# Gated layers: hidden activations of blocks 1 to 8 turned by 32x32 blocks on VectorE and exchanged through DRAM, instead of transposed on TensorE

## The reference

```python
D_FF = 2816
def _swiglu(x, w_in, w_out):
    g, u = jnp.split(x @ w_in, 2, axis=-1)
    return (jax.nn.silu(g) * u) @ w_out

h = _swiglu(_rms_norm(x, ffn1_pre_norm[l]), ffn1_w_in[l], ffn1_w_out[l])
x = x + 0.5 * _rms_norm(h, ffn1_post_norm[l])
m = _token_mixing(...)
x = x + _rms_norm(m, mix_post_norm[l])
h = _swiglu(_rms_norm(x, ffn2_pre_norm[l]), ffn2_w_in[l], ffn2_w_out[l])
x = x + 0.5 * _rms_norm(h, ffn2_post_norm[l])
```

## Time and profile before

| what | us |
|---|---|
| median of 3 runs | 1209.76 (1209.64 to 1209.85) |
| span of the profiled execution, first to last instruction | 1207.9 |
| median less span (start and end around the instructions) | 1.9 |
| TensorE matmul busy | 1197.5 (99%) |
| VectorE busy | 950.9 (79%) |
| ScalarE busy | 622.3 (52%) |
| GpSimd busy | 84.8 (7%) |
| moved by the transfers | 274.31 MB, mean 227 GB/s |
| granted TensorE clock, mean | 0.998 |

### The profile page before, as it was taken

One profiled execution on the slowest core, in us unless ns is written; L12 is line 12 of the kernel. 1 busy time (PEld: TensorE's weight loads), 2 busy tenths in 40 slices (PEclk: granted clock), 3 DMA queues, 4 the chain that ended last, 5 costly groups with the idle time before them and its releaser, 6 DMA issues.

```text
span 1207.9 us, 14813 instructions
## 1 busy us (share of the span) xinstructions
PE 1197.5 (99%) x5798; PEld 983.4 (81%) x5798; DVE 950.9 (79%) x1382; ACT 622.3 (52%) x851; POOL 84.8 (7%) x133
## 2 busy tenths in 40 slices
PE   9999999999999999999999999999999999999997
PEld 7888888888778888888887778888888788888885
DVE  7799868876766689888786668898898878765656
ACT  7445337445774363434465667444446576643441
POOL 2110130000300011000000000000100000000000
PEclk9999999999999999999999999999999999999999
DMA  9999996644645489899566437788856544566640
GB/s 317 347 337 322 307 302 192 218 142 154 203 152 174 152 297 355 309 328 316 172 208 206 139 105 263 271 304 280 309 196 241 192 141 139 177 219 214 188 161 35
DMA packets 145685, 274.31 MB, mean 227 GB/s; under 512 B 6336, under 2 KB 76432, under 8 KB 145616
## 3 DMA queue, kind: packets, MB, share of 16 engines
q1 hardware_dynamic: 127568, 209.73, 51.7%
q0 software_dynamic: 17888, 63.57, 15.4%
q10 hardware_dynamic: 160, 0.07, 0.0%
HBM read 270.41 MB, written 2.93 MB: 226 GB/s over the span
## 4 chain that ended last, share of the span: by engine, by line
PE 94%; DVE 2%; ACT 2%; issue 1%; DVEq 0%
PE ps L532 24%; PE ps L534 24%; PE ps L533 24%; PE ps L865 7%; PE ps L864 3%; PE ps L784 2%; PE ps L732 1%; PE ps L611 1%; ACT hi_w L1194 1%; PE ps L1081 1%; PE ps L738 1%; PE ps L1060 1%; PE ps L942 1%; PE ps L1058 1%; ACT area L1511 1%
## 5 line engine op out<-in xcount | busy, mean ns | idle before, releaser
L1707 DVE TENSOR_TENSOR lo_w<-w_raw,hi_w 128x2048 fp32r<-128x2048 f32 x194 | 440.9, 2286 | 60.9 <-ACT hi_w L1194 60.5
L1194 ACT ACTIVATE hi_w<-w_raw 128x2048 fp32r<-128x2048 f32 x195 | 370.2, 1915 | 51.4 <-DMA w_raw<-in_ffn_w_in 18.6
L532 PE MATMUL ps<-hi_w,xT 128*128 128x512 f32 x848 | 339.4, 400 | 0.0
L534 PE MATMUL ps<-lo_w,xT 128*128 128x512 f32 x848 | 331.3, 391 | 0.0
L533 PE MATMUL ps<-hi_w,xT 128*128 128x512 f32 x848 | 330.7, 390 | 0.0
L532 PEld LDWEIGHTS ps<-hi_w,xT 128*128 128x128 f32 x848 | 159.4, 188 | 36.3 <-issue 4.9
L532 PE MATMUL ps<-hi_w,hT_hi 128*128 128x512 f32 x480 | 188.5, 393 | 0.0
L534 PEld LDWEIGHTS ps<-lo_w,xT 128*128 128x128 f32 x848 | 159.2, 188 | 34.3
L534 PE MATMUL ps<-lo_w,hT_hi 128*128 128x512 f32 x480 | 187.1, 390 | 0.0
L533 PE MATMUL ps<-hi_w,hT_lo 128*128 128x512 f32 x480 | 187.0, 390 | 0.0
L533 PEld LDWEIGHTS ps<-hi_w,xT 128*128 128x128 f32 x848 | 159.6, 188 | 30.8
(11 more groups left out here) (321 smaller groups left out, 1152.1 us busy)
## 6 DMA issues: line engine op xcount, KB each, us to landing
w_raw<-in_ffn_w_in SPq DMA_DIRECT2D x86, 512.0 KB
aux<-in_ada_w POOLq DMA_DIRECT2D x34, 1024.0 KB, 7.5
w_raw<-in_mlp_w_up SPq DMA_DIRECT2D x32, 1024.0 KB
w_raw<-in_mlp_w_down SPq DMA_DIRECT2D x32, 1024.0 KB
w_raw<-in_w_mix_in SPq DMA_DIRECT2D x26, 1024.0 KB
w_raw<-in_ffn_w_out SPq DMA_DIRECT2D x22, 1024.0 KB
area<-in_ada_w POOLq DMA_DIRECT2D x14, 1024.0 KB, 5.6
w_raw<-in_moba_w_in SPq DMA_DIRECT2D x12, 1024.0 KB
```

The costliest lines, as they stand in the source:

```text
L532: pe.matmul(dst, lhs_hi, rhs_hi, start=start, stop=False)
L534: return pe.matmul(dst, lhs_hi, rhs_lo, start=False, stop=stop)
L1194: act.activation(hi_w[:, ring_slot(u), :], w_raw[:, ring_slot(u), :], ACT.Copy).then_inc(w_hi, 1)
L1707: vec.tensor_tensor(lo_w[:, ring_slot(u), :], w_raw[:, ring_slot(u), :], hi_w[:, ring_slot(u), :].bitcast(F32), ALU.subtract).then_inc(w_l ...
```

## The change

In blocks 1 to 8 of both gated layers (`moved(i)`) the four transposes on TensorE are left out. In their place:

- VectorE, straight behind `product`, turns `hid` (128 x 512 f32) in one instruction by 32x32 blocks into `hid_turned` (`turn_blocks`). Inside each block rows and columns have changed places; the blocks themselves have not.
- SP's queue writes `hid_turned` (256 KB) to DRAM scratch (`hidden_out`), waiting for `turn_blocks`, and reads it back in four transfers of 32 partitions each, in pieces of 128 f32, so that the blocks come to their places in `hid_raw` (`hidden_back`), waiting until the write has landed. Both stand in the order of the weights' loads: `hidden_out(i)` ahead of the down unit i+1, `hidden_back(i)` behind it.
- `hidden_hi` and `hidden_lo` read `hid_raw` in SBUF instead of PSUM, through a permuted pattern. ScalarE's `hidden_hi` moves behind the second `split_hi`, and waits for the reads; VectorE's `hidden_lo` moves behind the second half of the piece and the second `split_lo`.

```diff
+def moved(i):
+    return 1 <= i <= N_FF - 3
...
+        hid_dram = nc.dram_tensor("hidden_scratch", (2 * (N_FF - 3), P, 512), F32, kind="Internal").ap()
...
+        hid_turned, hid_raw = part(5120, 512), part(5632, 512)
...
+            def hidden_out(b):
+                n = moved_no(b)
+                sp.wait_ge(hid_blocks, n)
+                sp.dma_start(hid_dram[n - 1], hid_turned).then_inc(hid_saved, 16)
+
+            def hidden_back(b):
+                n = moved_no(b)
+                sp.wait_ge(hid_saved, 16 * n)
+                if b % N_FF > 1:
+                    sp.wait_ge(hidT_lo, b)
+                rows = hid_dram[n - 1].rearrange("(a i) (b r) -> b i a r", a=4, b=4)
+                for q in range(4):
+                    dst = hid_raw[32 * q:32 * q + 32, :].rearrange("p (a r) -> p a r", a=4)
+                    sp.dma_start(dst, rows[q]).then_inc(hid_landed, 16)
...
                 def step(u, i):
                     swiglu_in(u, w_in, i + 1, 0)
                     swiglu_in(u + 1, w_in, i + 1, 1)
+                    if i >= 2:
+                        hidden_out(b0 + i - 1)
                     out_unit(u + 2, i)
+                    if i >= 2:
+                        hidden_back(b0 + i - 1)
...
                     gate_up(u, b + 1, i + 1, 0)
-                    hidden_T(b, i, 2)
+                    if not moved(i):
+                        hidden_T(b, i, 2)
                     gate_up(u + 1, b + 1, i + 1, 1)
...
                 def hidden_hi(b, i):
-                    act.wait_ge(hidT, b + 1)
+                    hi, _, c0 = ffn_hT[i % 3]
+                    if moved(i):
+                        act.wait_ge(hid_landed, 64 * moved_no(b))
+                        act.activation(hi[:, c0:c0 + 2, :].rearrange("p c (t a j) -> p a (c t) j", t=NT, a=4),
+                                       hid_raw.rearrange("p (a x j) -> p a x j", a=4, x=4), ACT.Copy).then_inc(hidT_hi, 1)
+                        return
...
                     split_hi(u + LEAD)
-                    hidden_hi(b, i)
+                    if not moved(i):
+                        hidden_hi(b, i)
                     split_hi(u + LEAD + 1)
+                    if moved(i):
+                        hidden_hi(b, i)
                     activation(b + 1, i + 1)
...
+                if b < B_MLP1 and moved(i):
+                    h_lo, h_hi = (v[:, c0:c0 + 2, :].rearrange("p c (t a j) -> p a (c t) j", t=NT, a=4) for v in (lo, hi))
+                    vec.tensor_tensor(h_lo, hid_raw.rearrange("p (a x j) -> p a x j", a=4, x=4), h_hi.bitcast(F32),
+                                      ALU.subtract).then_inc(hidT_lo, 1)
+                    return
...
+                def turn_blocks(b):
+                    n = moved_no(b)
+                    vec.wait_ge(hid_done, b + 1)
+                    if n > 1:
+                        vec.wait_ge(hid_saved, 16 * (n - 1))
+                    vec.transpose(hid_turned.rearrange("p (b c t j) -> p t c b j", b=4, c=2, t=NT),
+                                  hid[:, :, 0:FF_B].rearrange("p t (c b i) -> p t c b i", c=2, b=4))\
+                       .then_inc(hid_blocks, 1)
...
                     split_lo(u + LEAD)
                     if piece is not None and i > 0:
                         piece_half(piece, 0, aux)
-                    hidden_lo(b, i, 2, ffn_hT[i % 3])
+                    if not moved(i):
+                        hidden_lo(b, i, 2, ffn_hT[i % 3])
                     if piece is not None and i == 0:
                         piece_half(piece, 0, aux)
                     if piece is not None:
                         piece_half(piece, 1, aux)
                     split_lo(u + LEAD + 1)
+                    if moved(i):
+                        hidden_lo(b, i, 2, ffn_hT[i % 3])
                     product(b + 1, i + 1)
+                    if moved(i + 1):
+                        turn_blocks(b + 1)
                     if piece is not None:
                         piece_fold(piece)
```

More of the change, by code:

```diff
@@ L146, with hidT_no, moved_no @@
 PIECES_A = 16
+def moved(i):
+    return 1 <= i <= N_FF - 3
+def hidT_no(b):
+    return sum(c >= B_MLP1 or not moved(c % N_FF) for c in range(b + 1))
+def moved_no(b):
+    return sum(moved(c % N_FF) for c in range(b + 1))
 def turned_up(j):
@@ L308, in two_blocks_kernel @@
         hidT, hidT_hi, hidT_lo = sem("hidT"), sem("hidT_hi"), sem("hidT_lo")
+        hid_blocks, hid_saved, hid_landed = sem("hid_blocks"), sem("hid_saved"), sem("hid_landed")
         up_low, up_sum, up_sq = sem("up_low"), sem("up_sum"), sem("up_squared")
@@ L398, in swiglu_in, with swiglu @@
                     sp.dma_start(dst[:, :, g, :], src).then_inc(w_landed[ring_slot(u)], 16)
-            def swiglu(u0, w_in, w_out):
+            def hidden_out(b):
[11 more added lines that the diff above has]
+                    sp.dma_start(dst, rows[q]).then_inc(hid_landed, 16)
+            def swiglu(u0, b0, w_in, w_out):
                 w_in = w_in.rearrange("(k p) (g f) -> p k g f", p=P, g=2)
@@ L421, in swiglu @@
                     swiglu_in(u0 + 2 * i + 8, w_in, i, 0)
+                    if i == N_FF - 1:
+                        hidden_back(b0 + N_FF - 4)
                     swiglu_in(u0 + 2 * i + 9, w_in, i, 1)
+                    if i == N_FF - 2:
+                        hidden_out(b0 + N_FF - 4)
                 for i in range(N_FF - 3, N_FF):
                     out_unit(u0 + 2 * N_FF + i, i)
+                    if i == N_FF - 3:
+                        hidden_out(b0 + i)
+                    if i == N_FF - 2:
+                        hidden_back(b0 + N_FF - 3)
             def mlp(u0, layer):
@@ L486, in _ @@
             quarter_in(1, 1)
-            swiglu(U_FFN1, d["ffn1_w_in"][0], d["ffn1_w_out"][0])
+            swiglu(U_FFN1, B_FFN1, d["ffn1_w_in"][0], d["ffn1_w_out"][0])
             w_mix = d["w_mix_in"][0].rearrange("(k p) n -> p k n", p=P)
@@ L502, in _ @@
                 square(u + 6 + i, w_mo, i % 2, i // 2)
-            swiglu(U_FFN2, d["ffn2_w_in"][0], d["ffn2_w_out"][0])
+            swiglu(U_FFN2, B_FFN2, d["ffn2_w_in"][0], d["ffn2_w_out"][0])
             qkv_out(U_MOBA, d["moba_w_in_2"][0], d["moba_w_out_2"][0])
@@ L1377, in hidden_hi @@
                 def hidden_hi(b, i):
-                    act.wait_ge(hidT, b + 1)
+                    act.wait_ge(hidT, hidT_no(b))
                     pair = 4 + 2 * (i % 2)
@@ L2043, in product @@
                     vec.wait_ge(act_done, b + 1)
-                    if i >= 1:
-                        vec.wait_ge(hidT, b)
+                    if i >= 1 and not moved(i - 1):
+                        vec.wait_ge(hidT, hidT_no(b - 1))
+                    if i >= 1 and moved(i - 1):
+                        vec.wait_ge(hid_blocks, moved_no(b - 1))
                     for t in range(NT):
```

2 lines of the change are left out of this document (1 added, 1 removed).

## The result

| | median us | runs | ratio to before, 95% interval |
|---|---|---|---|
| before | 1209.70 | 1209.39 to 1209.85 | |
| after | 1247.24 | 1242.34 to 1251.59 | 1.0309 [1.029, 1.0328] |

The change costs 37.5 us. The direction was forecast, the size was not: 1247 lies 21 us above the predicted 1226 and 7 us above the range.

A forecast was written before the change was run, and what follows sets the result against it. TensorE, holding 94% of the chain, was taken to bound the kernel. 1209.8 - 7.4 (transposes) + 17.0 (three late blocks) + 1.3 (settled blocks) + 1.5 (lateness) + 4.0 (clock) = 1226.2 us; predicted 1226, range 1214 to 1240.

The forecast's parts named there:

- The three late blocks: Down products of blocks 1 and 4, first layer, and block 1, second layer, wait for the later low part: 17.0 us.
- a late piece: Block 1, first layer: new transfers share the engines with the piece VectorE awaits; 1.1 us added, making its wait 6.8.
- where I had 1.3: Settled blocks: VectorE's path of 16.6 us against TensorE's 16.36; 0.12 us paid in some 11 blocks.
- the clock: TensorE's granted clock can fall in idle times of 4 to 5 us; about 2 us per return, 4 us in all.
- the lateness of the exchange and of the weights: Reads and weights arriving late through SP's queue and the transfer engines: 1.5 us in all, bounds 0 to 10.
- reads landed by 13 are in time for 14.7: Settled blocks: reads issued until 10.8 us, landed by about 13, needed by 14.7 for ScalarE's rounding ahead of hidden_lo.
- makes 1.01: First layer's transfer engines, busy for 0.98 at 345 GB/s, reach 1.01 with 0.5 MB more on 5.2 MB.
- The sign that I had named for it: ScalarE's waits for the reads exceeding 2 us in settled blocks would show rival (a).
- Rival (a): The exchange is late in most blocks: 1.5 us in 11 settled blocks adds 16, giving 1242 us; chance 0.20.
- is passed by nothing: Transfers: the exchange goes in the weights' own queue and nothing passes POOL's queue; no size was given.
- The saving: Four transposes gone from TensorE's chain in each of 16 moved blocks, 0.46 us each: 7.4 us, bounds 7.0 and 7.7.
- The 512-byte pieces: Reads of the exchange in 512-byte pieces, the least size at line rate, cost their bytes and no more.

The follow-up runs named there:

- the kernel with the order alone: Kernel before with only hidden_hi and hidden_lo of blocks 1 to 8 moved to their new places, transposes kept, no exchange: 1231.72 us, ratio 1.018.
- the traffic-only kernel: Kernel before, old order, transposes kept and used; turning, 256 KB write and reads added, their result unused: 1221.52 us, ratio 1.0092.
- the old places with 8 KB: Changed kernel with hidden_hi and hidden_lo in their old places, write cut to 8 KB, reads to 2 KB, blocks left unexchanged: 1207.17 us, ratio 0.9978.
- the square: Four kernels without the transposes: old places 1207.2 us with 8 KB written, 1232.7 with 256 KB; new places 1230.2 and 1247.2.
- the two kernels that take it away: Changed kernel without block 8's exchange, 1241.89 us; changed kernel with TensorE's block i+2 product waiting only for hid_done of a moved block, 1243.7 us.

## Why the prediction was wrong

**What held.** TensorE bounds the kernel and a wait costs its length: waits, clock and transposes add up to the change of the span within 0.4 us. The turning takes 712 ns (0.75 forecast) and adds nothing by itself (1.0007). The low parts are the releaser of nine of the eleven waits. The three late blocks were named and sized: 5.9, 6.8 and 4.3 us forecast, 4.7, 8.6 and 4.4 measured, 17.6 against 17.0 in sum. That the sum fits so well is in part luck: block 4 came out 1.2 us shorter and block 1 of the first layer 1.8 us longer. Its 8.6 hold the 1.9 us that VectorE waited for the reads' rounding, where I had added 1.1 for a late piece, and the low part's own 0.68 us, which I had left out: VectorE comes to it at 53.83 and then still has to do it, so with the hand-over the product could start at 54.8 and not at 54.1 (55.11 in the kernel with the order alone, which has no exchange). The order alone gave 1231.7 us with the transposes, and 1230.2 without them and with hardly any bytes. The latter stands against 1224.7 from the same terms of the forecast (1209.8 - 7.4 + 17.0 + 1.3 + 4.0); this part was 5.5 us too low. In the trace of that kernel four blocks outside the three wait 2.9 us, where I had 1.3, and the clock takes half of 12.2 us, where I had 4.0.

**The step that failed: the lateness of the exchange and of the weights.** "I take 1.5 us in all for such lateness, 0 to 10 as bounds." With the new places it measured 17.0 us (1247.2 against 1230.2 with 8 KB), the wait at block 10 and the clock behind the later waits included. Two readings stood behind the 1.5. One, that reads landed by 13 are in time for 14.7. Write and reads land 6.5 and 3.7 us after their issue, the reads later than the 2.2 us that I had between 10.8 and 13. And I had looked at the reads, not at what stands behind them in the queue: in the traffic-only kernel the weights of block 4 are issued 7.9 us later than before. Two, that 0.5 MB more on 5.2 MB "makes 1.01" of the engines' time: I wrote down that the engines would be more than full and then charged next to nothing for it. The bytes alone, unused, cost 11.6 us, above even the upper bound of 10. The sign that I had named for it, waits of ScalarE of over 2 us for the reads, is of no use, although it was there (86.8 us in 16 blocks, 5.4 each): in the old places with 8 KB ScalarE waits 118.3 us for them, 7.4 each, and that kernel is the only one that is faster than before. Rival (a), the exchange late in most blocks, named this mechanism, at 16 us in settled blocks and a chance of 0.20; its time of 1242 is 5.2 us below the median. It is the rival that came true on top of the forecast, but through fewer and longer waits than it said: the waits outside the four long ones are 35.1 - 26.2 = 8.9 us, not 1.5 us in each of 11 blocks. The reason given against it, that every wait of TensorE gives the transfers time, fits the 8.4 us of overlap in the square, and is not enough.

**The step that was left out.** Of the moved instructions I followed `hidden_lo` to the down product, but not `hidden_hi` and `hidden_lo` to the gate product two blocks on, which waits for the same semaphores for its PSUM pair. In block 10 of the first layer it stands 9.2 us in the profiled execution, some 3 to 6 us in the median of the two kernels that take it away. POOL's queue, of which I wrote that it "is passed by nothing", has its 1792 KB write in just this stretch, 16 us long in after and 15 without block 8's exchange or before. With 8 KB in the exchange POOL's write takes as long (15.1 us) and TensorE has no wait there. That the two compete for the transfer engines is read from the times of their landing and was not tried by itself.

**The size that was off: the clock.** "4 us, bounds 0 and 7": 11.9 us in the profiled execution. The estimate per long stall (about 2 us from the earlier trace rows) is near: two stretches cost 2.9 and 2.5 us (half of 5.85 and 4.94), and four short ones the other 6.5. What was wrong is their number, six instead of two, for the clock fell at stalls of 2.3 and 3.1 us as well (before 150.99 and 537.47 us on TensorE's timeline). But the clock is not a term that can be added by itself: kept busy, TensorE ran at 0.993 and the kernel was no faster than after by what can be told. Since the later waits bring clock losses of their own, the 17.0 us above and these 11.9 overlap.

**The saving.** Four transposes hold 0.44 us in the chain, and 64 of them 7.0. The saving was never seen in full: 1.5 us between the two kernels in the new order (1231.7 and 1230.2), 2.8 us in the best case. The old order with 8 KB shows reasons, in its own 3.6 us of waits and in 3.4 us of work at half clock behind the second of them (its profiled run is the slowest of its eleven). In block 1 of the first layer even reads of 2 KB, issued at 42.1 us, reach ScalarE only at 48.8. TensorE waits 1.4 us there. In block 4, behind `small_vectors`, VectorE works nearly without a pause up to the low part and TensorE waits 2.2 us for it:

```profile
100.94 0.68 DVE L2052 TENSOR_TENSOR hT_lo<-area,hT_hi 128x512 fp32r<-128x512 f32 x1
```

There VectorE was just in time for TensorE before, with its low part at 97.84. Now the low part starts 3.1 us later: its product of block 2 is already 1.5 us late behind block 1's reads (55.32 against 53.83), and the rest comes on from block to block, where VectorE has the turning to do and next to no time to spare. The Trainium skill (TensorE: Matmul & The Clock Gate, Part 4: PE-mode transpose) gives about 275 ns for one inside a kernel; the record of after is 273 ns for those that are left, and neither a saving of 17.6 us nor one of 7.4 can be found in any run here.

**The 512-byte pieces.** The Trainium skill (DMA: Bandwidth & Descriptors, Specifications) puts the least transfer at line rate at 512 bytes. The runs agree that the pieces have no price of their own that can be told: reads alone, in 512-byte pieces, and the write alone, in pieces of 2 KB, cost the same 1.8 us.

**Still open.** Write and reads together cost over three times the sum of the two alone. The traces show that the weights come later and that block 4 has little to spare; how much of the delay is the transfer engines moving more and how much is SP waiting for the write ahead of the next weights is open. A kernel whose exchange has a queue of its own that no engine with other work issues was not run. How the 17.0 us of the bytes divide between reads that are late and weights that are late was not measured with the new places.

No version that does the exchange beat the kernel before; the nearest are 10.9 us (three blocks of each layer) and 23 us (all eight, old places) slower.

## What to carry to other kernels

An exchange through DRAM must be priced not only by its own latency, but by what it delays, in the block that has least to spare: here 4.2 MB more fitted in for 1.8 us and 8.4 MB cost 12, most of it at one block, while the same number of tiny transfers cost nothing. A long wait of an engine that is busy for half of the time is not a sign of lateness; compare it with the same engine's waits before. When an instruction is moved to a later place so that its input is ready, follow every semaphore that it raises to all who wait for it, and compare with leaving it where it is: here the late input would have cost less than the late place, 14.6 us less. Before an engine that holds 94% of the chain is relieved of 0.46 us a block, see that the next engine has that much to spare in each block, the late ones above all.

## What the runs showed of the hardware that was not expected

- The granted clock fell to 0.50 at stalls as short as 2.3 and 3.1 us, and TensorE worked on at half speed for 3.1 to 5.9 us after each of six stalls (rows of the six stretches above). The earlier trace rows had suggested stalls of 4 to 5 us. Not every such stall does it: with the exchange in three blocks one of 3.1 us (before 504.91 us) left the clock at 1.00.
- The transfer engines' share went over 1 (1.06 and 1.09 at 337 and 366 GB/s in short stretches), and a share of 1.00 from 110 to 170 us went with 323 GB/s with the reads alone and 347 with the whole traffic, while TensorE lost nothing in either. The share is not a measure of what room is left.
- POOL waited 14.8 us (before) to 17.0 us (traffic only) for its 1792 KB write to DRAM beside the weights, 108 to 124 GB/s.
- The same 256 KB write landed in 8.3 us (traffic-only kernel), 7.0 (write alone), 6.5 (after) and 5.3 us (old places). It lands soonest where the engines that take the weights are themselves held back, though no run tried this by itself.
